# The first mixture of a two-layer float32 kernel: one gather for two experts' first 64 rows, layer two in four column quarters on partition strips, and the spread by strips

## The chip, the cores and the metric

The kernel runs on one core of a Trainium2 chip. The metric is the time of one execution on the device, in microseconds; lower is better. Four engines matter here: TensorE (PE in the profile) multiplies matrices, VectorE (DVE) and ScalarE (ACT) work element by element, SyncE (SP) issues the loads of the weights. Matrices are float32 all through.

## What is computed

Two transformer-like blocks in a row on 256 tokens of width 1024. The first ends with a mixture of 32 experts, and this mixture is all that the change touches:

```python
def moe_ffn(h, w_router, b_router, w1, b1, w2, b2):      # T = 256 tokens, D = 1024
    top_v, top_e = lax.top_k(logits, TOP_K)              # 4 of 32 experts a token
    weights = jax.nn.softmax(top_v, axis=-1)
    ...
    def expert_block(args):                              # the rows of one expert
        tok, e = args
        hcat = x_pad[tok] @ w1[e] + b1[e]                # 1024 -> 2048, "layer one"
        x_glu = jnp.minimum(hcat[:, ::2], SWIGLU_LIMIT)
        x_lin = jnp.clip(hcat[:, 1::2], -SWIGLU_LIMIT, SWIGLU_LIMIT)
        act = x_glu * jax.nn.sigmoid(SWIGLU_ALPHA * x_glu) * (x_lin + 1.0)
        return act @ w2[e] + b2[e]                       # 1024 -> 1024, "layer two"
    ...
    out = jnp.sum(y[dest].reshape(T, TOP_K, D) * weights[..., None], axis=1)
```

How many of the 256 tokens an expert gets is known only from the data; with the inputs here no expert gets more than 96.

## The kernel before, in words

`tensor_moe1` is the TensorE part of the first mixture. It loops over the experts u = 0 to 31, written out one after another in the program. An expert's rows are taken in passes of 32 rows. The code of four passes (128 rows) is in the program for every expert; passes two, three and four stand in `If(count > 32)`, `If(count > 64)`, `If(count > 96)`, where `count` is loaded into a register of TensorE (L914). Where an `If` is not taken, TensorE branches over the code of the further passes. `either` (L746) adds an `Else` that raises the semaphore, `only` (L736) has none.

For one expert TensorE does, in this order:

- **Layer one, half 0**: bias through a 32x32 matmul (L874, four), then 16 matmuls (L881) of 32 rows by 512 columns, four strips of 32 PSUM partitions wide; they use chunks 0 and 1 of w1. The further passes' code follows in an `If`. **Half 1** is the same with chunks 2 and 3, without bias.
- **The spread of expert u - 1** (`spread1`, `spread`, L481): four matmuls of 128 x 512 add the expert's rows back to the tokens, each row times its weight; four more (L843) in an `If(count > 64)` for rows 64 to 127. VectorE adds the eight PSUM tiles into `YV` (`vector_spread`, L1748).
- **at**: two transpositions (L906) of the activation that VectorE has made out of layer one (L1825 to L1835, with the sigmoid of ScalarE, L2389).
- **The gather of expert u + 1** (`gather`): four transpositions of the weighted selection (L800, tile `swt`) and 16 matmuls of 128 x 128 (L481, tile `hg`) that pick the expert's rows, up to 128, out of the normalised tokens. ScalarE copies the results to SBUF (L2351, L2368).
- **Layer two**: 16 matmuls (L893) of 32 rows by 512 columns for pass 0, the further passes in `If`s (L962 and below). ScalarE copies each pass's result to SBUF in two pieces of 64 x 512 (L2400, `evict`, all four passes always).

SyncE loads six chunks of 2 MB an expert (four of w1, two of w2) into a ring of eight slots, in program order. A slot is loaded anew when TensorE has freed its last chunk (semaphores `s_pe`, `s_px`, `s_py`).

In both programs TensorE's instructions stand in memory in the order of the code, with all bodies of `If`s between them.

## Time and profile before

| | before |
|---|---|
| time of three executions, us | 2183.54, 2178.27, 2179.35 (median 2179.35) |
| span of the profiled execution, first to last instruction, us | 2180.7 |
| TensorE busy, share of the span | 83% |
| mean granted TensorE clock | 0.927 |
| first mixture's experts, us from the span's start | about 392 to 1397 |
| weights loaded for them | 192 loads of 2048 KB |

The profile gives no time of the profiled execution beside its span; the span lies 1.35 us above the median of the three executions, so that a sum made in the span's microseconds can be taken over to the median with that shift. A timeline row reads: start, duration, engine, line, operation, tiles, shapes, number of records, and in brackets how long the engine had stood idle ahead of it and what it waited for.

### The profile page before, as it was taken

The page shows a single profiled execution, that of the slowest core. Times are in us where ns is not written, and L with a number is a line of the kernel's source. Part 1 is how long each engine was busy: PE and PEld are TensorE (multiplying, and loading weights), DVE is VectorE, ACT ScalarE, POOL GpSimd, SP SyncE. Part 2 cuts the span into 40 slices and gives each one's busy share as a digit, 9 for nine tenths or more (in the row PEclk, how much of TensorE's full clock was granted, in tenths as well). Part 3 has the DMA queues.
Part 4 walks back from the last instruction along what each step waited for, and adds up shares of the span by engine and source line. Part 5 has one row for each costly group of instructions (what it writes and reads, how often), then busy time and mean ns, then how long its engine had stood idle before and what let it go on. Part 6 is the DMA issues. An engine that isn't in the chain of part 4 may idle for free. (4 is left out here: it accounts for less than half of the span.)

```text
span 2180.7 us, 28331 instructions
## 1 busy us (share of the span) xinstructions
PE 1818.2 (83%) x11496; PEld 831.2 (38%) x11496; DVE 806.8 (37%) x1613; ACT 506.2 (23%) x1028; POOL 77.0 (4%) x96
## 2 busy tenths in 40 slices
PE   7899999999999988989977898599989855565556
PEld 3654445433333433434333243255534522222221
DVE  2215533333342434534444344488882200000001
ACT  2022311232331233332333333222410200000000
POOL 0000000000000000000000000085000000000000
PEclk9999999999999999999999999799999878877888
DMA  7835349789897799999999999534228299999997
GB/s 268 301 133 195 136 173 376 316 367 409 342 420 311 309 425 423 422 423 402 425 422 423 423 424 423 189 121 142 91 102 345 96 429 428 427 428 428 428 427 320
DMA packets 114821, 713.56 MB, mean 327 GB/s; under 512 B 16799, under 2 KB 21102, under 8 KB 69006
## 3 DMA queue, kind: packets, MB, share of 16 engines
q1 hardware_dynamic: 106208, 704.98, 79.3%
q10 hardware_dynamic: 8398, 5.47, 0.9%
q8 instruction: 165, 2.70, 0.5%
q14 instruction: 50, 0.41, 0.1%
HBM read 709.35 MB, written 1.07 MB: 326 GB/s over the span
## 5 line engine op out<-in xcount | busy, mean ns | idle before, releaser
L881 PE MATMUL ps<-ring,ar 128*32 128x512 f32 x3072 | 368.3, 620 | 41.7 <-DMA ring<-in_w 18.4
L481 PE MATMUL ps<-ar 128*128 128x128 f32 (+5 forms) x1742 | 351.2, 359 | 41.0 <-PEq L755 20.5
L488 PE MATMUL ps<-ring,ar 128*32 128x512 f32 x1184 | 196.0, 691 | 138.0 <-DMA ring<-in_w_gate 45.3
L481 PEld LDWEIGHTS ps<-ar 128*128 128x128 f32 (+2 forms) x1742 | 234.1, 200 | 160.5 <-issue 121.8
L481 PE MATMUL ps<-ring,ar 128*128 128x512 f32 (+2 forms) x592 | 248.8, 580 | 3.8 <-DVE ar L1423 1.7
L881 PEld LDWEIGHTS ps<-ring,ar 128*32 128x32 f32 x3072 | 99.3, 113 | 307.5 <-issue 279.9
L1825 DVE TENSOR_SCALAR ar<-ps 128x256 f32<-128x256 f32 x128 | 54.4, 425 | 403.8 <-PE ps L881 395.0
L893 PE MATMUL ps<-ring,ar 128*32 128x512 f32 x1536 | 175.0, 602 | 0.0
L596 PE MATMUL ps<-ring,ar 128*128 128x512 f32 x384 | 170.2, 594 | 0.0
L481 PEld LDWEIGHTS ps<-ring,ar 128*128 128x128 f32 x592 | 113.2, 193 | 132.8 <-issue 127.0
L2400 ACT ACTIVATE ar<-ps 64x512 f32<-64x512 f32 x256 | 151.3, 591 | 46.6 <-PE ps L893 33.4
L1748 DVE TENSOR_TENSOR ar<-ps,ar 128x512 f32<-128x512 f32 x176 | 121.7, 692 | 101.6 <-PE ps L481 91.2
L488 PEld LDWEIGHTS ps<-ring,ar 128*32 128x32 f32 x1184 | 55.7, 125 | 246.2 <-issue 245.3
L488 PE MATMUL ps<-ar 128*32 128x512 f32 x288 | 112.2, 703 | 37.6 <-DMA ring<-in_w_up 21.8
L2389 ACT ACTIVATE ar<-ar 128x256 f32<-128x256 f32 x128 | 53.3, 416 | 315.8 <-DVE ar L1825 309.8
L1835 DVE TENSOR_TENSOR ar<-ar 128x256 f32<-128x256 f32 x128 | 79.5, 621 | 97.5 <-ACT ar L2389 90.7
L2437 ACT ACTIVATE ar<-ps 128x256 f32<-128x256 f32 x128 | 49.0, 383 | 256.9 <-PE ps L906 208.0
L2124 DVE TENSOR_TENSOR ar<-ps,ar 128x512 f32<-128x512 f32 x8 | 5.5, 692 | 262.0 <-ACT ar L2576 262.0
L596 PEld LDWEIGHTS ps<-ring,ar 128*128 128x128 f32 x384 | 71.2, 191 | 79.8 <-issue 79.4
L893 PEld LDWEIGHTS ps<-ring,ar 128*32 128x32 f32 x1536 | 46.5, 111 | 101.3 <-issue 101.3
L2368 ACT ACTIVATE ar<-ps 128x512 f32<-128x512 f32 x80 | 47.8, 597 | 94.9 <-PE ps L481 94.9
L874 PE MATMUL ps<-ar 32*32 32x512 f32 x384 | 53.8, 617 | 15.2 <-PEq L973 10.5
(403 smaller groups left out, 1385.8 us busy)
## 6 DMA issues: line engine op xcount, KB each, us to landing
ring<-in_w SPq DMA_DIRECT2D x192, 2048.0 KB, 20.0
ring<-in_w_gate SPq DMA_DIRECT2D x25, 2048.0 KB, 29.4
ring<-in_w_up SPq DMA_DIRECT2D x25, 2048.0 KB, 31.4
ring<-in_w_down SPq DMA_DIRECT2D x24, 2048.0 KB, 30.1
ring<-in_w_in SPq DMA_DIRECT2D x21, 2048.0 KB, 8.7
ring<-in_w_ada SPq DMA_DIRECT2D x12, 2048.0 KB, 8.5
ar<-in_w_up SPq DMA_DIRECT2D x7, 2048.0 KB, 29.2
ar<-in_w_gate SPq DMA_DIRECT2D x7, 2048.0 KB, 29.6
```

The lines of the kernel that those rows point to most:

```text
L481: ins = self.t.e.matmul(o, l, r, start=(i == 0), stop=(i == len(pairs) - 1))
L488: ins = self.t.e.matmul(b[32 * i:32 * i + 32, :], l, r, start=(k == 0), stop=(k == len(steps) - 1))
L596: ins = t.e.matmul(b[:, :], HV[:, k, TB(tb)], W[:, k, :], start=(k == 0), stop=(k == 7))
L874: e.matmul(b[32 * s:32 * s + 32, :], pick, B1R[:, HALF(s)], start=True, stop=False)
L881: ins = e.matmul(b[32 * s:32 * s + 32, :], HG[:, 2 * c + r, 32 * n:32 * n + 32], W[:, r, HALF(s)], start=False, stop=(c == 3 and r == 1))
L893: ins = e.matmul(b[64 * h + 32 * r:64 * h + 32 * r + 32, :], AT_[:, 2 * s + r, 32 * n:32 * n + 32], W[:, s % 2, r, HALF(h)], start=(s == 0 ...
L1748: k = v(v.own.tensor_tensor(o, b, o, ALU.add))
L1825: dve["glu", u, n] = v(v.own.tensor_scalar(glu, b[:, 0:512:2], 7.0, None, ALU.min))
L1835: dve["ac", u, n] = v(v.own.tensor_tensor(o, lin.rearrange("p (q r) -> p q r", r=2), sg.rearrange("p (q r) -> p q r", r=2), ALU.mult))
L2389: act["sg", u, n] = s(s.own.activation(M[:, 512:768], M[:, 0:256], ACT.Sigmoid, scale=1.702))
L2400: k = s(s.own.activation(YG_[n // 2][64 * (n % 2):64 * (n % 2) + 64, HALF(h)], ps("l2", u, n)[64 * h:64 * h + 64, :], ACT.Copy))
L2437: m = s(s.own.activation(o, ps("at", u, k)[:, 256 * i:256 * i + 256].rearrange("p (r s n) -> p r s n", r=2, s=4), ACT.Copy))
```

## The change

Layer two of a pass writes four column quarters of 256 onto the four strips of 32 partitions of one PSUM bank (32 matmuls of 256 columns in place of 16 of 512), so ScalarE evicts a pass with one copy of 128 x 256. The spread multiplies strip by strip: for every pass eight matmuls of 32 rows deep by 256 columns wide, passes two to four in `If`s, and it stands between the two halves of layer one in place of behind them. For the weights, a selection is turned by matmuls of 32 x 128 that write each pass onto all four strips (`turned_picks`). The gather is made once for two experts, for 64 rows of each (`gather_pair`, in odd experts only); rows 64 to 127 are gathered in an `If(count > 64)` inside the expert itself (`rest`). VectorE picks two experts ahead, and adds the spread at the start of an expert, ahead of its four activation steps; ScalarE copies what `rest` made for every expert, taken or not. The activation has one buffer (`ATB`) in place of two.

```diff
-    ATB = [A(2048 + 1024 * i, 8, 128) for i in range(2)]
-    ACB, YG_ = A(4096, 4, 256), [A(5120 + 1024 * i, 1024) for i in range(2)]
-    SB = [A(7168 + 256 * i, 2, 128) for i in range(2)]
-    SWB = A(7680, 2, 2, 128)
-    SWT = [A(8192 + 512 * i, 2, 256) for i in range(2)]
-    TM = [A(9216 + 768 * i, 768) for i in range(2)]
+    ATB = A(2048, 8, 128)
+    ACB, YG_ = A(3072, 4, 256), A(4096, 4, 256)
+    SB = [A(5120 + 512 * i, 2, 2, 128) for i in range(2)]
+    SWB = [A(6144 + 256 * i, 2, 128) for i in range(2)]
+    SWT = [A(6656 + 1024 * i, 4, 256) for i in range(2)]
+    TM = [A(8704 + 768 * i, 768) for i in range(2)]
+    HGR = A(10240, 8, 64)
...
-    TL1X = (7, 0)
+    QUART = (4, 5, 6, 7)
...
-    def gather_weights(t, w, m, u, lane):
-        b = w.claim("swt", m, u, lane=lane)
-        t.wait_ge(s_dve, dve["sel", m, u])
-        for i in range(2 if m == 1 else 1):
+    def turned_picks(t, b, u, passes):
+        for i, n in enumerate(passes):
             for tb in range(2):
-                ins = t.e.transpose(b[:, TB(2 * i + tb)], (SWB, SWB2)[m - 1][:, i, tb, :], ident)
-        pe["swt", m, u] = t(ins)
-    def gather_rows(t, w, m, u, lane):
-        t.wait_ge(s_dve, dve["pick", m, u])
-        t.wait_ge(s_act, act["rows", m])
+                for q in range(4):
+                    ins = t.e.matmul(b[32 * q:32 * q + 32, TB(2 * i + tb)], SWB[u % 2][:, tb, 32 * n:32 * n + 32],
+                                     ident, start=True, stop=True)
+        return ins
+    def gather_pair(t, w, p, h, lane):
+        t.wait_ge(s_dve, dve["pick", 1, 2 * p + 1])
+        t.wait_ge(s_act, act["rows", 1])
+        b = w.claim("hg", 1, p, h, lane=lane)
+        for k in range(4):
+            n = w.sums(b[:, TB(k)], [(XNV[:, tb, TB(4 * h + k)], SB[p % 2][:, :, tb, 0:64]) for tb in range(2)])
+        pe["hg", 1, p, h] = n
+    def gather_turned(t, w, u, lane):
+        b = w.claim("swt", 1, u, lane=lane)
+        t.wait_ge(s_dve, dve["sel", 1, u])
+        pe["swt", 1, u] = t(turned_picks(t, b, u, (0, 1)))
...
     def tensor_moe1(t, w):
         e = t.e
         tensor_route(t, w, 1, WR1, 32, 128)
-        gather_rows(t, w, 1, 0, TL1)
-        gather_weights(t, w, 1, 0, TL1)
+        for h in range(2):
+            gather_pair(t, w, 0, h, (TL1[h],))
+        gather_turned(t, w, 0, (6,))
...
         def spread1(u, count):
-            spread(t, w, 1, u, TL1)
-            def second_half():
-                t.wait_ge(s_act, act["yg", 1, u, 1])
+            banks4 = [w.claim("sp", 1, u, q, lane=(QUART[q],)) for q in range(4)]
+            def rows(n):
+                t.wait_ge(s_act, act["yg", 1, u, n])
                 for tb in range(2):
-                    for h in range(2):
-                        b = w.claim("sp", 1, u, 1, tb, h, lane=TL1X)
-                        psp[u, tb, h] = z(e.matmul(b[:, :], SWT[u % 2][:, 1, TB(tb)], YG_[1][:, HALF(h)], start=True,
-                                                   stop=True))
-            either(t, z, count, 64, second_half)
-            psp["all", u] = z.n
+                    for q in range(4):
+                        g = slice(32 * q, 32 * q + 32)
+                        ins = e.matmul(banks4[q][:, 256 * tb:256 * tb + 256], SWT[u % 2][g, n, TB(tb)], YG_[g, n, :],
+                                       start=(n == 0 and tb == 0), stop=True, skip_group_check=True)
+                return ins
+            def third():
+                only(t, count, 96, lambda: rows(3))
+                rows(2)
+            def second():
+                only(t, count, 64, third)
+                z(rows(1))
+            pe["sp", 1, u] = t(rows(0))
+            either(t, (z,), count, 32, second)
+            psp[u] = z.n
...
+            def rows_of(k, n):
+                if n < 2:
+                    c0 = 64 * (u % 2) + 32 * n
+                    return HGB[u // 2 % 2][:, k, c0:c0 + 32]
+                return HGR[:, k, 32 * n - 64:32 * n - 32]
...
+            def layer2(b, n, halves, arrive, first):
 
                 for s in range(4):
+                    if s // 2 not in halves:
+                        continue
                     if arrive and s % 2 == 0:
                         w.weights("w2", u, s // 2)
                     W = RG_(slot["w2", u, s // 2], 0, 2, 2, 1024)
-                    for h in range(2):
-                        for r in range(2):
-                            ins = e.matmul(b[64 * h + 32 * r:64 * h + 32 * r + 32, :],
-                                           AT_[:, 2 * s + r, 32 * n:32 * n + 32], W[:, s % 2, r, HALF(h)],
-                                           start=(s == 0), stop=(s == 3))
+                    for r_ in range(2):
+                        for q in range(4):
+                            ins = e.matmul(b[32 * q:32 * q + 32, 0:256], ATB[:, 2 * s + r_, 32 * n:32 * n + 32],
+                                           W[:, s % 2, r_, 256 * q:256 * q + 256], start=(s == 0 and r_ == 0),
+                                           stop=(s == 3 and r_ == 1))
...
+                def rest():
+                    b = w.claim("hr", u, lane=(3,))
+                    for k in range(8):
+                        for tb in range(2):
+                            e.matmul(b[:, 64 * k:64 * k + 64], XNV[:, tb, TB(k)], SB[u // 2 % 2][:, u % 2, tb, 64:128],
+                                     start=(tb == 0), stop=(tb == 1))
+                    b = w.claim("sr", u, lane=(2,))
+                    r(turned_picks(t, b, u, (2, 3)))
 
                 def further(n):
                     if half == 0:
                         w.claim("l1", u, n, lane=(n,))
-                    return layer1(ps("l1", u, n), n, half, False)
+                    return layer1(ps("l1", u, n), n, chunks, False)
 
                 def third():
+                    t.wait_ge(s_act, act["rest", u])
                     only(t, count, 96, lambda: further(3))
                     further(2)
 
                 def second():
+                    if half == 0:
+                        either(t, (r,), count, 64, rest)
+                        w.claim("l1", u, 1, lane=(1,))
+                    b1 = ps("l1", u, 1)
+                    layer1(b1, 1, chunks[0:1], False)
                     only(t, count, 64, third)
-                    x(further(1))
-                either(t, x, count, 32, second)
-                for c in (2 * half, 2 * half + 1):
+                    x(layer1(b1, 1, chunks[1:2], False))
+                either(t, (x, r), count, 32, second)
+                if half == 0:
+                    pr["rest", u] = r.n
+                for c in chunks:
                     w.free("w1", u, c)
                     px["free", "w1", u, c], py["free", "w1", u, c] = x.n, 0
+                if half == 0 and u > 0:
...
+                    spread1(u - 1, counts[u - 1])
             px["l1", u] = x.n
-            if u > 0:
-                spread1(u - 1, counts[u - 1])
             if u == LATE_BIAS:
                 biases()
-            pe["at", u, 0] = t(turn_act(0, (0,)))
+            further_pair = u % 2 == 1 and u + 1 < NE
             if u + 1 < NE:
-                gather(t, w, 1, u + 1, TL1)
-            turn_act(1, (1,))
+                gather_turned(t, w, u + 1, (5,))
+            if further_pair:
+                gather_pair(t, w, u // 2 + 1, 0, (6,))
+            pe["at", u, 0] = t(turn_act(0, (0,), 4))
+            if further_pair:
+                gather_pair(t, w, u // 2 + 1, 1, (4,))
             t.wait_ge(s_act, act["at", u, 0])
 
             def first_second(ins):
@@ -947,30 +1013,26 @@
             def first_third(ins):
                 px["at", u, 2] = x(ins)
 
-            pe["l2", u, 0] = t(layer2(w.claim("l2", u, 0, lane=(7,)), 0, True, first_second))
+            b = w.claim("l2", u, 0, lane=(7,))
+            layer2(b, 0, (0,), True, None)
+            turn_act(1, (1,), 5)
...
+            pe["l2", u, 0] = t(layer2(b, 0, (1,), True, first_second))
...
+    def vector_quarters(v, u):
+        v.wait_ge(s_pe, pe["sp", 1, u])
+        v.wait_ge(s_ps, psp[u])
+        for q in range(4):
+            o = YV[:, :, 256 * q:256 * q + 256]
+            b = ps("sp", 1, u, q).rearrange("p (b n) -> p b n", b=2)
+            if u == 0:
+                v(v.own.tensor_copy(o, b))
+            else:
+                v(v.own.tensor_tensor(o, b, o, ALU.add))
+            read["sp", 1, u, q] = v.mark()
...
         for u in range(NE):
             if u + 1 < NE:
-                vector_pick(v, 1, u + 1)
                 vector_select(v, 1, u + 1)
+            if u + 2 < NE:
+                vector_pick(v, 1, u + 2)
+            if u > 0:
+                vector_quarters(v, u - 1)
...
-                if n == 0 and u > 0:
-                    vector_spread(v, 1, u - 1)
-                    if u == LATE_BIAS:
-                        biases()
-        vector_spread(v, 1, NE - 1)
+                if n == 0 and u == LATE_BIAS:
+                    biases()
+        vector_quarters(v, NE - 1)
...
+    def scalar_rest(s, u):
+        s.wait_ge(s_pr, pr["rest", u])
+        if u > 0:
+            s.wait_ge(s_px, px["l1", u - 1])
+        if u > 1:
+            s.wait_ge(s_pe, pe["sp", 1, u - 2])
+            s.wait_ge(s_ps, psp[u - 2])
+        s(s.own.activation(HGR, ps("hr", u).rearrange("p (k s) -> p k s", k=8), ACT.Copy))
+        read["hr", u] = s.mark()
+        act["rest", u] = s(s.own.activation(SWT[u % 2][:, 2:4, :], ps("sr", u).rearrange("p (n q) -> p n q", n=2),
+                                            ACT.Copy))
+        read["sr", u] = s.mark()
...
-            for h in range(2):
-                k = s(s.own.activation(YG_[n // 2][64 * (n % 2):64 * (n % 2) + 64, HALF(h)],
-                                       ps("l2", u, n)[64 * h:64 * h + 64, :], ACT.Copy))
+            act["yg", 1, u, n] = s(s.own.activation(YG_[:, n, :], ps("l2", u, n)[:, 0:256], ACT.Copy))
...
         for u in range(NE):
+            scalar_rest(s, u)
             sigmoid(u, 0)
+            if u + 1 < NE:
+                scalar_gather_turned(s, u + 1)
+            if u % 2 == 1 and u + 1 < NE:
+                scalar_gather_pair(s, u // 2 + 1, 0)
             turned_act(s, u, 0, (0,))
-            if u + 1 < NE:
-                scalar_gather(s, 1, u + 1, l1, lambda: sigmoid(u, 1))
-            else:
-                sigmoid(u, 1)
+            sigmoid(u, 1)
+            if u % 2 == 1 and u + 1 < NE:
+                scalar_gather_pair(s, u // 2 + 1, 1)
             turned_act(s, u, 1, (1,))
             for n in (2, 3):```

TensorE in expert 1 before, from the end of layer one's half 1 to the first pass of layer two (L752 the Else of layer one, L481 of 128x512 the spread, L843 its second half, L906 the turned activation, L800 `swt`, L481 of 128x128 the gather `hg`, L893 layer two):

```order
L752 UNCONDITIONAL_BRANCH
L481 MATMUL ps<-ar 128x512 x4
L748 COMPARE_AND_BRANCH
L843 MATMUL ps<-ar 128x512 x4
L748 UNCONDITIONAL_BRANCH
L752 UNCONDITIONAL_BRANCH
L906 MATMUL ps<-ar 128x128 x2
L800 MATMUL ps<-ar 128x128 x4
L481 MATMUL ps<-ar 128x128 x16
L906 MATMUL ps<-ar 128x128 x2
L893 MATMUL ps<-ring,ar 32x512 x16
```

TensorE in expert 1 after, between layer one's half 0 (ends with the two branches of L749 and L753) and half 1 (L922), where L869 is the spread:

```order
L753 UNCONDITIONAL_BRANCH
L869 MATMUL ps<-ar 128x256 x8
L749 COMPARE_AND_BRANCH
L741 COMPARE_AND_BRANCH x2
L869 MATMUL ps<-ar 128x256 x8
L741 UNCONDITIONAL_BRANCH
L869 MATMUL ps<-ar 128x256 x8
L741 UNCONDITIONAL_BRANCH
L869 MATMUL ps<-ar 128x256 x8
L749 UNCONDITIONAL_BRANCH
L753 UNCONDITIONAL_BRANCH
L922 MATMUL ps<-ring,ar 32x512 x16
```

The spread has moved up from behind half 1 to between the halves, and is one group of eight and three more in nested `If`s where it was four and four. TensorE in expert 1 after, from layer one's end to layer two (L803 the turned selection, L482 the gather for two experts, L949 the turned activation, L936 layer two):

```order
L753 UNCONDITIONAL_BRANCH
L803 MATMUL ps<-ar 32x128 x16
L482 MATMUL ps<-ar 128x128 x8
L949 MATMUL ps<-ar 128x128 x2
L482 MATMUL ps<-ar 128x128 x8
L936 MATMUL ps<-ring,ar 32x256 x16
L949 MATMUL ps<-ar 128x128 x2
L936 MATMUL ps<-ring,ar 32x256 x16
L749 COMPARE_AND_BRANCH
```

Between layer one and the turned activation there stands the gather's first part, and the second turned activation has moved into the middle of layer two, whose matmuls are 32 in place of 16. TensorE in expert 1 after, from the start of layer one's half 0 to the end of its `If`s' first part (L915 bias, L965 and L803 of `rest`):

```order
L915 MATMUL ps<-ar 32x512 x4
L922 MATMUL ps<-ring,ar 32x512 x16
L749 COMPARE_AND_BRANCH x2
L965 MATMUL ps<-ar 128x64 x16
L803 MATMUL ps<-ar 32x128 x16
L749 UNCONDITIONAL_BRANCH
L753 UNCONDITIONAL_BRANCH
L915 MATMUL ps<-ar 32x512 x4
L922 MATMUL ps<-ring,ar 32x512 x8
```

Where before the further passes followed at once, the body of `rest` now stands ahead of them; the four further groups of layer two, counted like this through one expert, make 368 matmuls in the program on average (360 in even, 376 in odd experts), where the expert had 244.

## Rows read from the trace of the kernel before

**Rows 1.** The page: queue with instructions (packets, MB, share); loads (KB each, us to landing)

```profile
q8 instruction: 165, 2.70, 0.5%
...
ring<-in_w SPq DMA_DIRECT2D x192, 2048.0 KB, 20.0
```

**Rows 2.** Windows: busy us and (records) of each engine, PEclk, DMA share, GB/s

```profile
390.00:740.00 350.00, 331.36 (x2669) 129.16 (x2667) 126.67 (x264) 97.66 (x190) 0.00 (x0) 1.00 0.86 356
740.00:1372.00 632.00, 552.29 (x3934) 226.32 (x3926) 258.83 (x535) 206.05 (x403) 0.00 (x0) 0.95 1.00 419
```

**Rows 3.** Instruction groups, 385 to 1400 us: busy us, mean ns, idle before

```profile
L881 PE MATMUL ps<-ring,ar 128*32 128x512 f32 x3072 | 368.3, 620 | 41.7 <-DMA ring<-in_w 18.4 <-issue 12.3 <-PEq L755 10.7
...
L481 PE MATMUL ps<-ar 128*128 128x512 f32 x256 | 130.4, 653 | 27.7 <-PEq L755 20.5 <-ACT ar L2400 3.6 <-ACT ar L2389 2.7
...
L881 PEld LDWEIGHTS ps<-ring,ar 128*32 128x32 f32 x3072 | 99.3, 113 | 307.5 <-issue 279.9 <-DMA ring<-in_w 27.3
```

**Rows 4.** TensorE's waits, 385 to 1400 us: total, times, longest

```profile
PE ps L874 <- PEq L973: 10.5, 4, 2.9
```

**Rows 5.** TensorE timeline of expert 23 (its start to that of expert 24)

```profile
1120.51 1.06 PE L874 MATMUL ps<-ar 32*32 32x512 f32 x8 [2.85 <-PEq L973]
...
1126.21 3.64 PE L881 MATMUL ps<-ring,ar 128*32 128x512 f32 x32 [1.07 <-PEq L755]
1131.87 5.37 PE L481 MATMUL ps<-ar 128*128 128x512 f32 x8 [2.03 <-PEq L755]
...
1138.03 3.84 PE L481 MATMUL ps<-ar 128*128 128x128 f32 x32
...
1142.35 3.64 PE L893 MATMUL ps<-ring,ar 128*32 128x512 f32 x32
1145.92 1.06 PE L874 MATMUL ps<-ar 32*32 32x512 f32 x8
```

**Rows 6.** TensorE timeline in expert 24 and at its end

```profile
1149.40 3.62 PE L881 MATMUL ps<-ring,ar 128*32 128x512 f32 x26 [1.43 <-issue]
1156.06 5.34 PE L881 MATMUL ps<-ring,ar 128*32 128x512 f32 x32 [3.04 <-PEq L755]
1161.98 1.09 PE L481 MATMUL ps<-ar 128*128 128x512 f32 x2 [0.58 <-PEq L755]
```

**Rows 7.** TensorE timeline: first and last of twelve pairs of stalls

```profile
425.49 3.64 PE L881 MATMUL ps<-ring,ar 128*32 128x512 f32 x32 [0.57 <-PEq L755]
431.40 1.10 PE L481 MATMUL ps<-ar 128*128 128x512 f32 x2 [2.27 <-PEq L755]
...
1336.73 5.34 PE L881 MATMUL ps<-ring,ar 128*32 128x512 f32 x32 [4.26 <-PEq L755]
1342.61 0.67 PE L481 MATMUL ps<-ar 128*128 128x512 f32 x1 [0.54 <-PEq L755]
```

**Rows 8.** TensorE timeline: starts of experts 1, 2, 10, 11 and 31

```profile
420.29 1.06 PE L874 MATMUL ps<-ar 32*32 32x512 f32 x8
...
443.75 1.06 PE L874 MATMUL ps<-ar 32*32 32x512 f32 x8
...
739.49 1.06 PE L874 MATMUL ps<-ar 32*32 32x512 f32 x8
...
766.21 1.06 PE L874 MATMUL ps<-ar 32*32 32x512 f32 x8 [2.15 <-PEq L973]
...
1355.58 1.06 PE L874 MATMUL ps<-ar 32*32 32x512 f32 x8
```

**Rows 9.** TensorE timeline: matmuls 32 rows deep, and of 256 columns

```profile
1508.52 1.17 PE L481 MATMUL ps<-ring 32*128 32x256 f32 x16
...
1609.07 1.93 PE L488 MATMUL ps<-ring 128*32 128x256 f32 x32
```

**Rows 10.** TensorE timeline, the last spread of the first mixture

```profile
1390.27 6.48 PE L481 MATMUL ps<-ar 128*128 128x512 f32 x8 [3.59 <-ACT ar L2400]
```

**Rows 11.** The chain that ended last, VectorE behind expert 31's sums

```profile
1398.02 2.96 issue
```

More of the change, by code:

```diff
@@ L1132, in tensor_moe2 @@
         tensor_route(t, w, 2, W36, 36, 32)
-        gather(t, w, 2, 0, TL2)
+        gather(t, w, 0, TL2)
         for u in range(NE // 4):
@@ L2373, in scalar_moe1 @@
+            read["hg", 2, u, h] = s.mark()
+        act["hg", 2, u] = n
     def scalar_moe1(s):
```

238 lines of the change are left out of this document (113 added, 125 removed).

## The prediction

> **What bounds the kernel now.** The change touches the first mixture alone, so I read its stretch, 385 to 1400 us, by windows, by groups, by waits, and then expert by expert on TensorE. The windows show two parts [rows 2]. From 390 to 740 us the DMA share is 0.86 and TensorE is busy for 331 of 350 us. From 740 to 1372 us the DMA share is 1.00 at 419 GB/s, and TensorE is busy for 552 of 632. There the loads set the pace: six of 2048 KB [rows 1] at 419 GB/s are 30.0 us an expert, and experts 11 to 31 start 589.4 us apart over 20 experts, 29.5 each [rows 8]. TensorE has some 80 us to spare in this part.
>
> The groups and the waits ask for a second look. Little of TensorE's idle time is for data (18.4 us for weights); 20.5, 10.7 and 10.5 us are its sequencer behind the `Else`s of L755 and L973, and 12.3 us are "issue" in the middle of layer one [rows 3, 4]. A branch does not explain the latter: no branch stands there. What does is where they stand. Layer one's 48 passes of 32 matmuls left 3072 MATMUL and 3072 LDWEIGHTS records [rows 3], so a matmul is four queue entries and a transposition two; an expert before is 244 matmuls (12 of them transpositions) and some 20 branches, 977 entries. Counted in these entries along the program, all eight gaps inside layer one (the one at 1149.40 is one) [rows 6] lie at the same place modulo 256. The page has a queue that moved 165 packets of instructions, 2.70 MB [rows 1], 16.4 KB each, 64 bytes times 256. And walking TensorE's program with the branches that this data takes touches 165 blocks of 256 entries. So TensorE's program comes in blocks of 256 entries, and an engine that enters a block early waits for it.
>
> How long a block takes is seen where two stalls follow each other over one block boundary: from one resumption to the next there is one block. Expert 23 resumes at 1120.51, 1126.21 and 1131.87: 5.70 and 5.66 us; expert 24 at 1149.40, 1156.06 and 1161.98: 6.66 and 5.92 [rows 5, 6]. Over twelve such pairs in the stretch, of which the first and the last stand in [rows 7] with 5.91 and 5.88, the mean is 6.1. The packets share the DMA engines with the loads; VectorE's jump at the end of the stretch, with few loads under way, shows 2.96 us [rows 11], which I take for the low end.
>
> **The change part by part, as work.** The spread before costs 130.4 us for 32 experts, 4.1 each [rows 3]. Sixteen records 32 rows deep and 256 columns wide took 1.17 us [rows 9], so after it is 1.2 a pass, 1.8 an expert: -2.3. The gather was 3.84 an expert [rows 5], after it is half as often: -1.9. Layer two takes 3.64 a pass [rows 5]; 64 records of 256 columns are twice 1.93 [rows 9]: +0.2. `rest` adds a gather of 3.8 for three-pass experts alone (5), and ahead of their third pass a wait for two ScalarE copies. Net TensorE work falls by 3 to 4 us in a one-pass expert, and rises by 1 in a three-pass one. In the part from 740 on the loads hide that saving. Before 740 the DMA engines stand still for 0.14 of 350 us [rows 2], 49 us, mostly beside the experts of three passes, whose work does not fall: I count -4. Behind expert 31 the spread falls from 6.48 [rows 10] to 1.2 us, and its copies and sums shorten with it: -9. VectorE's and ScalarE's edits (picks two ahead, sums first, one copy a pass, the two copies of `rest` always) lie beside TensorE; if that cover were gone they would cost the sums' 2.8 us at the start of an expert. Work alone gives 2181 - 4 - 9 + 1 = 2169.
>
> **The change as program.** Per expert the code grows from 244 to 368 matmuls, 977 to 1486 entries, 3.8 to 5.8 blocks: +64 blocks in 32 experts. Not taken bodies are skipped. Before, no jump was over 245 entries, less than a block, so nothing was ever passed by. After, a one-pass expert jumps over 92 matmuls (376 entries) in half 0 and over 100 (400) behind layer two. Such a jump passes a whole block in (376-255)/256 and (400-255)/256 of cases, together 1.0 an expert, for 21 one-pass experts 21 blocks. So 165 + 64 - 21 = 208 blocks.
>
> A one-pass expert thus walks 4.8 blocks in place of 3.8. At 6.1 us that is 23.2 us before; the five in the first part took 23.5 to 26.7, mean 25.1 (the first and the last of them in [rows 8]), so the surplus over the fetch is 1.9. After, 4.8 x 6.1 = 29.3, and with 1.7 of surplus 31.0. That is over the 29.5 of the loads: from there on the instructions, not the weights, set the pace. Two-pass experts enter the `If`s and jump shorter, 5.7 blocks, 35 us; three-pass ones walk 5.6, 34 us, hidden under some 48 us of work.
>
> The Trainium skill, page "Runtime: NRT & Kernel Launch", section "Instruction fetch mechanics", gives blocks of 256 instructions, purely sequential prefetch, and a stall where a taken branch leaves the two blocks at hand. The trace agrees with the 256 [rows 1]; no jump before is long enough to show the stall. By its rule of the jump the sum would be the one below. The same section calls the crossing of a block mostly hidden, by which it would be that of rival 1; the resumptions in [rows 5, 6] say otherwise.
>
> The sum, by parts:
> - Experts 0 to 10: five of one pass, 31.0 in place of 25.1, +29; four of three passes +2 each (1 of work, 1 of the wait for `rest`), +8; the two of two passes 0.
> - Experts 11 to 30: 15 x 31.0 + 4 x 35 + 48.5 = 653 in place of 589: +64.
> - The end: -9 of work, +4 for one more block: -5.
> Together +96 on a span of 2180.7, which is 1.35 above the median: 2275.
>
> Bounds. With 5.7 us a block, the short end of the pairs, a one-pass expert takes 29.1: the parts are +20 + 8 + 36 - 6 (two-pass experts at 35 still) and the time 2237; with no surplus 27.4, the loads' 29.5 bind again, and the parts are +12 + 8 + 17 - 6 (two- and three-pass experts alone are longer) and the time 2210. If the block that is jumped over has been asked for already and must land first, up to 5.8 blocks count; in half the cases that is +3 us in 21 experts, less what overlaps, +50: 2325. I take 6.1, the mean of the pairs, since the loads after are as dense as before.
>
> **The rivals.**
> 1. Faster, by the work. Block arrival is hidden, or a jump is served as quickly as a fall-through. For it: TensorE stood idle only some 55 us for its sequencer over the whole stretch [rows 3, 4]. Against: three resumptions 5.7 us apart in one expert [rows 5]. It gives 2169, 0.5% faster. It decides if a block takes under 3 us, as in [rows 11]. Chance 0.08.
> 2. No change. A block takes 3 to 4.5 us; a one-pass expert then stays under the loads' 29.5, the work's -12 is eaten by the stalls after far jumps (21 x 0.5 to 1 us). 2180, within 6. For it: the loads bound 632 us of the stretch. Chance 0.07.
> 3. Slower, but less: 5 to 5.7 us a block, because TensorE's longer waits leave the loads gaps in which blocks come sooner. 2215 to 2245. Chance 0.25.
> 4. My forecast, 2245 to 2310. Chance 0.45.
> 5. Slower still: the far jump waits for the block in flight and then for its own. 2310 to 2350. Chance 0.15.
>
> **How the numbers follow.** The likeliest is 2275. The range 2215 to 2335 leaves out rivals 1 and 2 (0.15) and the outer part of 5 (0.05), 2 in 10. A difference under 0.3% cannot be told from none here. Faster 0.08, same 0.07, slower 0.85.
>
> **What would show it.** The instruction queue: 165 packets become about 208 (up to 229 if passed blocks are fetched too), 2.70 MB becomes 3.4. One-pass experts start 29 to 33 us apart, before 740 and behind. TensorE's busy share from 740 on falls below 0.8, the DMA share below 1.00, and the idle time in front of the spread, of half 1 and of the next expert's bias is put down to the sequencer or to "issue", some 3 times as much as before. The last spread takes under 2 us. If the packets rise and the spacing does not, the 6.1 us is not what an early engine waits for, and the prediction falls; if the packets stay at 165, the count of blocks does.

## The result, and the profile after

| | before | after |
|---|---|---|
| median (lowest to highest), us | 2179.28 (2178.27 to 2183.54) | 2322.29 (2313.18 to 2327.66) |
| ratio after to before, 95% interval | | 1.0641 (1.0615 to 1.0668) |
| span of the profiled execution, us | 2180.7 | 2319.3 |
| first TensorE work behind the mixture, us | 1408.45 | 1547.89 |

The changed kernel is 6.4% slower by the ratio, and the medians lie 143 us apart (6.6%, inside the interval). The whole loss lies in the first mixture: the next stage's first work on TensorE comes 139.4 us later, of 138.6 us of span.

The page after: TensorE's busy time, the granted clock in 40 slices, and the queue that brings instructions (packets, MB, share).

```profile
PE 1794.5 (77%) x14208; PEld 862.2 (37%) x14208; DVE 772.2 (33%) x1529; ACT 423.6 (18%) x932; POOL 77.4 (3%) x96
...
PEclk9999998899989989879987789879999987787787
...
q8 instruction: 228, 3.74, 0.6%
```

Where [rows 1] had 165 packets there are 228, one under the upper figure of the prediction (229) and 20 above its likeliest (208), and TensorE's share has fallen from 83% to 77% though it executes more. The windows after (columns as in [rows 2]):

```profile
390.00:740.00 350.00, 289.37 (x3284) 135.84 (x3287) 100.59 (x207) 65.28 (x144) 0.00 (x0) 0.92 0.80 320
740.00:1360.00 620.00, 465.19 (x4766) 204.96 (x4758) 204.47 (x413) 125.56 (x281) 0.00 (x0) 0.87 0.89 361
```

From 740 us on TensorE's share is 0.75 and the DMA share 0.89, where [rows 2] had 0.87 and 1.00: the loads no longer set the pace, and no wait of TensorE for a load is left in the stage. The groups and then the waits of the stage (us in total, times, longest) say what does:

```profile
L922 PE MATMUL ps<-ring,ar 128*32 128x512 f32 x3072 | 409.8, 675 | 27.1 <-issue 14.3 <-PEq L758 12.8
...
L915 PE MATMUL ps<-ar 32*32 32x512 f32 x384 | 66.5, 749 | 102.4 <-PEq L758 96.7 <-issue 5.7
...
L869 PE MATMUL ps<-ar 32*128 32x256 f32 x768 | 67.4, 481 | 58.8 <-PEq L758 37.4 <-issue 15.7 <-ACT ar L2514 5.7
```

```profile
PE ps L915 <- PEq L758: 96.7, 24, 6.0
PE ps L869 <- PEq L758: 37.4, 13, 4.7
...
PE ps L869 <- issue: 15.7, 6, 3.5
PE ps L803 <- issue: 15.6, 5, 4.0
PE ps L922 <- issue: 14.3, 10, 2.8
```

All waits of TensorE for its sequencer and "issue" in the stage add up to 208 us (10 rows, of which these are the largest) against 59 before (7 rows, [rows 3, 4] have the largest). They stand in front of the next expert's bias (L915, behind the skip of layer two's further passes), of the spread (L869, behind the skip in half 0), and, as "issue", in the middle of straight code. The end of expert 16 and the whole of expert 17 on TensorE's timeline, both of one pass:

```profile
1010.75 2.21 PE L936 MATMUL ps<-ring,ar 128*32 128x256 f32 x32
1018.44 1.93 PE L915 MATMUL ps<-ar 32*32 32x512 f32 x8 [5.49 <-PEq L758]
1020.30 4.90 PE L922 MATMUL ps<-ring,ar 128*32 128x512 f32 x32
1028.75 1.19 PE L869 MATMUL ps<-ar 32*128 32x256 f32 x16 [3.54 <-PEq L758]
1029.87 1.06 PE L922 MATMUL ps<-ring,ar 128*32 128x512 f32 x1
1032.99 5.38 PE L922 MATMUL ps<-ring,ar 128*32 128x512 f32 x31 [2.06 <-issue]
1040.86 1.08 PE L803 MATMUL ps<-ar 128*32 128x128 f32 x32 [2.49 <-PEq L758]
...
1049.30 1.93 PE L936 MATMUL ps<-ring,ar 128*32 128x256 f32 x32
1055.62 1.93 PE L915 MATMUL ps<-ar 32*32 32x512 f32 x8 [4.39 <-PEq L758]
```

Read it as in [rows 5]. Expert 17 resumes at 1018.44, then at 1028.75 behind the long skip of half 0, 10.3 us later, where a pair before took 6.1; then at 1032.99 in straight code and at 1040.86 behind half 1's skip. It takes 37.2 us, of which the engine works about 24. The row of 1018.44 shows a second thing: eight records that take 1.06 us [rows 5] took 1.93 behind a wait of 5.49. The stretch's granted clock is 0.92 and 0.87 (PEclk in the windows) where it was 1.00 and 0.95 [rows 2], and layer one's 3072 records rose from a mean of 620 ns [rows 3] to 675. What the engine did ahead of this slow row is wait; the clock is examined below.

The end of the stage:

```profile
1532.15 2.09 PE L869 MATMUL ps<-ar 32*128 32x256 f32 x16 [5.75 <-ACT ar L2514]
1547.89 3.67 PE L571 MATMUL ps<-ar 128*128 128x128 f32 x16 [13.65 <-DVE ar L1461]
```

The last spread took 2.09 us where [rows 10] had 6.48, and from the start of expert 31 to the next stage's first work it is 47.6 us where it was 52.9.

### The profile page after: what moved, and what is told of

Read it like the earlier page. It is cut to its first block and busy times, and to the rows that moved or that the text cites. A ratio compares the mean times of both kernels' runs of the same rounds, so it can differ in the third digit from the quotient of the medians.

```text
span 2319.3 us, 33403 instructions
## 1 busy us (share of the span) xinstructions
PE 1794.5 (77%) x14208; PEld 862.2 (37%) x14208; DVE 772.2 (33%) x1529; ACT 423.6 (18%) x932; POOL 77.4 (3%) x96
## 3 DMA queue, kind: packets, MB, share of 16 engines
q8 instruction: 228, 3.74, 0.6%
HBM read 709.35 MB, written 1.07 MB: 306 GB/s over the span
## 5 line engine op out<-in xcount | busy, mean ns | idle before, releaser
L922 PE MATMUL ps<-ring,ar 128*32 128x512 f32 x3072 | 409.8, 675 | 27.1 <-issue 14.3
L489 PE MATMUL ps<-ring,ar 128*32 128x512 f32 x1184 | 193.9, 685 | 142.0 <-DMA ring<-in_w_gate 46.4
L1829 DVE TENSOR_TENSOR ar<-ps,ar 128x512 f32<-128x512 f32 x124 | 85.7, 691 | 498.2 <-PE ps L869 416.4
L482 PE MATMUL ps<-ring,ar 128*128 128x512 f32 (+2 forms) x592 | 246.7, 576 | 3.5 <-DVE ar L1485 1.7
L922 PEld LDWEIGHTS ps<-ring,ar 128*32 128x32 f32 x3072 | 103.5, 122 | 327.4 <-issue 327.2
L936 PE MATMUL ps<-ring,ar 128*32 128x256 f32 x3072 | 188.8, 394 | 11.7 <-ACT ar L2514 11.7
L482 PE MATMUL ps<-ar 128*128 128x128 f32 (+6 forms) x974 | 172.6, 338 | 26.3 <-ACT ar L2514 13.7
L482 PEld LDWEIGHTS ps<-ring,ar 128*128 128x128 f32 x592 | 112.3, 191 | 131.3 <-issue 125.7
L482 PEld LDWEIGHTS ps<-ar 128*128 128x128 f32 (+3 forms) x974 | 135.5, 214 | 64.0 <-issue 36.6
L489 PEld LDWEIGHTS ps<-ring,ar 128*32 128x32 f32 x1184 | 54.2, 124 | 250.2 <-issue 249.3
L915 PE MATMUL ps<-ar 32*32 32x512 f32 x384 | 66.5, 749 | 102.4 <-PEq L758 96.7
L936 PEld LDWEIGHTS ps<-ring,ar 128*32 128x32 f32 x3072 | 95.8, 113 | 83.0 <-ACT ar L2514 16.0
L869 PE MATMUL ps<-ar 32*128 32x256 f32 x768 | 67.4, 481 | 58.8 <-PEq L758 37.4
L2182 DVE TENSOR_TENSOR ar<-ps,ar 128x512 f32<-128x512 f32 x8 | 5.5, 692 | 263.0 <-ACT ar L2653 263.0
L869 PEld LDWEIGHTS ps<-ar 32*128 32x128 f32 x768 | 48.3, 228 | 90.1 <-issue 79.6
L2514 ACT ACTIVATE ar<-ps 128x256 f32<-128x256 f32 x128 | 49.2, 384 | 150.4 <-PE ps L936 90.0
## 6 DMA issues: line engine op xcount, KB each, us to landing
ring<-in_w SPq DMA_DIRECT2D x192, 2048.0 KB, 13.0
ring<-in_w_gate SPq DMA_DIRECT2D x25, 2048.0 KB, 29.4
ring<-in_w_up SPq DMA_DIRECT2D x25, 2048.0 KB, 31.4
ring<-in_w_down SPq DMA_DIRECT2D x24, 2048.0 KB, 30.1
ring<-in_w_in SPq DMA_DIRECT2D x21, 2048.0 KB, 8.1
ring<-in_w_ada SPq DMA_DIRECT2D x12, 2048.0 KB, 8.6
ar<-in_w_up SPq DMA_DIRECT2D x7, 2048.0 KB, 30.4
ar<-in_w_gate SPq DMA_DIRECT2D x7, 2048.0 KB, 29.4
```

Source lines behind the costliest of these rows:

```text
L482: ins = self.t.e.matmul(o, l, r, start=(i == 0), stop=(i == len(pairs) - 1))
L489: ins = self.t.e.matmul(b[32 * i:32 * i + 32, :], l, r, start=(k == 0), stop=(k == len(steps) - 1))
L869: ins = e.matmul(banks4[q][:, 256 * tb:256 * tb + 256], SWT[u % 2][g, n, TB(tb)], YG_[g, n, :], start=(n == 0 and tb == 0), stop=True, ski ...
L915: e.matmul(b[32 * s:32 * s + 32, :], pick, B1R[:, HALF(s)], start=True, stop=False)
L922: ins = e.matmul(b[32 * s:32 * s + 32, :], rows_of(2 * c + r_, n), W[:, r_, HALF(s)], start=False, stop=(c == 3 and r_ == 1))
L936: ins = e.matmul(b[32 * q:32 * q + 32, 0:256], ATB[:, 2 * s + r_, 32 * n:32 * n + 32], W[:, s % 2, r_, 256 * q:256 * q + 256], start=(s == ...
```

## The experiments

The first four were run side by side (median of the kernel before 2179.47 us), the others in two later groups (2181.66 and 2181.60). `only(t, count, 96, ...)` is a body that no expert here executes. The first three pad the kernel before with matmuls in such bodies.

**pad_near: 64 matmuls an expert that are never executed, no skip longer than a block**

```diff
+                def padding():
+                    for _ in range(55):
+                        e.matmul(ps("sp", 1, u, 1, 0, 0)[:, :], SWT[u % 2][:, 1, TB(0)], YG_[1][:, HALF(0)], start=True,
+                                 stop=True)
                 for tb in range(2):
                     for h in range(2):
                         b = w.claim("sp", 1, u, 1, tb, h, lane=TL1X)
+                        if tb == 0 and h == 0:
+                            only(t, count, 96, padding)
...
             def fourth():
+                b3 = w.claim("l2", u, 3, lane=(3,))
+                for _ in range(9):
+                    e.matmul(b3[0:32, :], AT_[:, 0, 96:128], RG_(slot["w2", u, 0], 0, 2, 2, 1024)[:, 0, 0, HALF(0)],
+                             start=True, stop=True)
...
```

> The kernel before with 64 more matmuls an expert in the program that are never executed (they stand under a condition of over 96 rows), placed so that no branch skips more than 245 entries: one block of 256 entries more an expert, no work more. Theory one (TensorE's instructions come in blocks of 256 entries, one after the other, some 5 to 6 us each): instruction packets 165 + 32 = 197, a one-pass expert walks 4.8 blocks, some 30 us, the time is 50 to 100 us above before. Rival (the changed kernel is slower by its work, its waits or the narrower matmuls, and the length of the program costs nothing): no change, 2179 within 6.

Measured: 2240.86 us against 2179.47, ratio 1.0296 (1.0272 to 1.0320), so +61 us.

```profile
q8 instruction: 197, 3.23, 0.6%
```

197 packets, as worked out. Instructions that are never executed cost 61 us; the rival falls. The bias rows of the timeline give each expert's start: the 20 one-pass experts from 1 to 30 are now 29.4 us apart on average, where they were 26.3.

**pad_far: the same 64, all in half 0's body of pass four**

```diff
                     if half == 0:
                         w.claim("l1", u, n, lane=(n,))
+                        for _ in range(64 if n == 3 else 0):
+                            e.matmul(ps("l1", u, n)[0:32, :], pick, B1R[:, HALF(0)], start=True, stop=False)
```

> The same 64 matmuls an expert, but all in one body that is always skipped, so that one branch an expert skips 501 entries and nearly always passes a whole block. Theory one with passed blocks fetched all the same: 197 packets, and as slow as the other placing or slower (60 to 120 us above before), since the jump waits for the block under way and then for its own. Theory one without such a fetch: 166 packets, and only the exposed time behind the jump, 20 to 60 us above before. Rival: no change.

Measured: 2305.36 us, ratio 1.0589 (1.0567 to 1.0611), +126 us, just above the 60 to 120 that I gave.

```profile
q8 instruction: 194, 3.18, 0.6%
```

The same number of packets within three, and twice the price: the block that is passed is fetched all the same, and it is not the number of blocks alone that counts but where they lie. The starts of the experts show where the second half of the price arises. One-pass experts, which skip the padding with everything else, are 29.8 us apart, hardly more than with the near placing (29.4). Two-pass experts (without expert 0) take 39.9 us in place of 33.7 and three-pass experts 52.0 in place of 47.0: they stop in front of a further pass of half 0, where the skip of the padding lands (14 waits of L874 put down to "issue", 40.1 us in all, 3.9 before). The eleven experts of two and three passes hold 61 of the 70 us by which the two placings differ between the starts of experts 0 and 31.

**pad_full: 124 matmuls an expert, skips as long as after's.** The same three places with 32 (half 0), 44 (spread) and 48 (layer two).

> The kernel before with 124 never executed matmuls an expert, as many as the change adds, and with skips of about the same lengths (377, 195, 200 and 405 entries): the work of before in a program as long as after. Theory one: 229 packets as after has 228, and 120 to 170 us above before, that is within 30 of after. Rival: no change, 2179 within 6.

Measured: 2327.37 us, ratio 1.0698 (1.0668 to 1.0729), +148 us; the changed kernel is at +143. Its queue and layer one's group:

```profile
q8 instruction: 227, 3.72, 0.6%
```

```profile
L889 PE MATMUL ps<-ring,ar 128*32 128x512 f32 x3072 | 405.9, 676 | 43.8 <-PEq L755 37.6 <-issue 6.2
```

This is the central run. It does the work of before, with the tiles, copies and waits of before, in a program as long as after's, and has after's time within 5 us and its packets (227). Layer one's records also have after's mean (676 ns, after 675). Its granted clock fell too, but less than after's: 0.95 and 0.92 in the two windows, where before had 1.00 and 0.95 and after has 0.92 and 0.87.

```profile
390.00:740.00 350.00, 302.95 (x2310) 114.00 (x2304) 111.90 (x235) 89.16 (x173) 0.00 (x0) 0.95 0.81 322
740.00:1360.00 620.00, 500.98 (x3390) 200.41 (x3382) 227.25 (x469) 170.62 (x335) 0.00 (x0) 0.92 0.90 366
```

So waits for instructions alone lowered the clock here, by 0.05 and 0.03 where the changed kernel lost 0.08 in both windows. That the rest of the fall is no cause of its own is not shown; before_no34 and after_no34 below come back to it.

**after_no4: the changed kernel without pass four's matmuls**

```diff
-                only(t, count, 96, lambda: rows(3))
                 rows(2)
...
-                    return layer1(ps("l1", u, n), n, chunks, False)
+                    return layer1(ps("l1", u, n), n, chunks, False) if n < 3 else None
...
-                layer2(w.claim("l2", u, 3, lane=(3,)), 3, (0, 1), False, None)
+                w.claim("l2", u, 3, lane=(3,))
```

> The changed kernel without the matmuls of pass four (rows 96 to 127, which no expert has with these inputs, so nothing that is executed is left out): 292 matmuls an expert in place of 368, 4.6 blocks in place of 5.8, and skips of 296 and 272 entries in place of 376 and 400. Theory one: packets 228 - 38 = 190, one-pass experts 28 to 30 us apart, the time 2180 to 2225. Rival (work, waits or narrow matmuls): nothing changes, 2322 within 8.

Measured: 2202.33 us, ratio 1.0110 (1.0093 to 1.0127).

```profile
q8 instruction: 190, 3.11, 0.6%
```

120 us of the 143 are gone with code that no expert executes; 190 packets, as worked out. One-pass experts are 27.4 us apart (28 to 30 expected). Three-pass experts still take 50.4 us, where before has 47.3: the shorter program does not take these 3 us each, 16 in all, back. `rest` alone is 4.9 us of work in each of them (L965 and L803, at 547.12 us in the changed kernel's expert 4).

**after_split: the long skips cut in two**

```diff
-                    if half == 0:
-                        either(t, (r,), count, 64, rest)
-                        w.claim("l1", u, 1, lane=(1,))
...
+                if half == 0:
+                    either(t, (r,), count, 64, rest)
-                either(t, (x, r), count, 32, second)
+                either(t, (x,), count, 32, second)
...
-                either(t, (y,), count, 64, third)
-            either(t, (x, y), count, 32, second)
+            either(t, (x,), count, 32, second)
+            either(t, (y,), count, 64, third)
```

> The changed kernel with the same matmuls in the same order, but its two long skips cut in two: the gather of rows 64 to 127 and the rest of half 0's further passes stand under two conditions one after the other (128 and 245 entries), and so do pass two and passes three and four of layer two (about 140 and 261). Same work, same length of program, some branches more. Theory one (blocks of 256 entries; passing a block costs its fetch and then the fetch of the next one): 228 packets as before the cut, and the time falls by 40 to 80 us, to about 2260, since the two paddings differed by 65 us for that reason alone. Rival (only the number of blocks fetched counts): 2322 within 10. Rival (work and waits): 2322, or a little above for the branches.

Measured: 2331.60 us, ratio 1.0686 (1.0658 to 1.0714): 9 us above the changed kernel, which was measured in another group; the intervals of the two ratios overlap at their edges, so that a loss is not certain. The 40 to 80 less that I had expected are ruled out. In this kernel the length of a skip as such has no price that cutting it takes away. **after_no4_split** is the same cut in the kernel without pass four:

> The changed kernel without pass four's matmuls and with its long skips cut in two as well: 4.6 blocks an expert, no skip over 255 entries. Theory one: 190 packets, one-pass experts at 27 to 29 us, so that the loads set the pace from 740 us on again: 2165 to 2185, against 2202 with the long skips. Rival (only the number of blocks counts): 2202 within 6.

Measured: 2212.13 us, ratio 1.0141 (1.0118 to 1.0165), 10 us above after_no4, with intervals that overlap, and outside both the 2165 to 2185 and the rival's 2202 within 6: the same miss. **pad_far_split** puts the padding of pad_far behind half 0 under a condition of its own:

```diff
                 either(t, x, count, 32, second)
...
+                if half == 0:
+                    only(t, count, 96, padding)
```

> The padding of 64 never executed matmuls an expert behind half 0, under a condition of its own, so that the one skip of 501 entries becomes two, of 245 and 258, that follow each other at once. If a long skip has a price of its own (the rule that a branch beyond the two blocks at hand must ask anew): about 2240, as the near placing. If what counts is that two blocks in a row hold no work, so that the time of the second block is not covered by anything (the theory left after the changed kernel did not gain by the same cut): 2305 within 12, as the far placing, with 194 to 197 packets.

Measured: 2290.57 us, ratio 1.0500 (1.0467 to 1.0534), 15 us below pad_far and 50 above pad_near. Just outside the 12 us that I gave, and far from 2240. Its largest wait on TensorE (us in total, times, longest):

```profile
PE ps L881 <- issue: 136.4, 37, 9.9
```

Single waits reach 9.9 us, more than any block took before. That fits two blocks in a row with no work between them, the second of which is asked for when the engine lands in the first. But the cut also moved the padding behind the further passes of half 0, and the starts of the experts show both effects: three-pass experts fall from 52.0 to 46.8 us and two-pass ones from 39.9 to 36.7, while one-pass experts rise from 29.8 to 31.4. So the 15 us gained are those of a better place, and do not speak for shorter skips.

**pad_jump: one skip over eight blocks among loads, one behind them**

```diff
                 t.wait_ge(s_act, act["yg", 1, u, 1])
+                for _ in range(512 if u in (15, NE - 1) else 0):
+                    e.matmul(ps("sp", 1, u, 0, 0, 0)[:, :], SWT[u % 2][:, 1, TB(0)], YG_[1][:, HALF(0)], start=True,
+                             stop=True)
```

> The kernel before with 512 never executed matmuls (2048 entries, eight blocks) in the skipped body of one spread among dense loads (that of expert 15's rows) and 512 in the last one, where few loads run. It reads off the price of one block directly. If every passed block is fetched in turn: 165 + 16 = 181 packets, some 8 x 5.5 = 44 us of stall in expert 16 and 8 x 3 = 24 us behind the last spread. If only the next block is fetched ahead and the engine then goes to the target: 165 to 167 packets and stalls of at most 12 and 6 us.

Measured: 2188.57 us, ratio 1.0032 (1.0014 to 1.0049). The queue, and TensorE at the skip, which stands between the spread (L481) and the turned activation (L909) of expert 16:

```profile
q8 instruction: 169, 2.77, 0.5%
```

```profile
916.98 7.07 PE L884 MATMUL ps<-ring,ar 128*32 128x512 f32 x64
926.41 5.37 PE L481 MATMUL ps<-ar 128*128 128x512 f32 x8 [2.35 <-PEq L755]
935.62 0.41 PE L909 MATMUL ps<-ar 128*128 128x128 f32 x2 [3.84 <-PEq L755]
```

Four packets more: that is two above what I gave for fetching one block ahead, and far from 16. Eight blocks are not fetched one after the other. The engine resumes at 926.41 and, behind the skip, at 935.62: 9.2 us, in place of the 5.7 to 6.7 of [rows 5, 6]. The whole of expert 16 took 31.9 us where it took 24.9 before, so the 3 us more at the skip are not all that this expert lost. Behind the last spread no stall showed: the next work on TensorE, which waits 11.5 us for VectorE there anyway, was not held up. The reading that fits, from this one skip, is that a long skip costs the rest of the block under way and then the target's.

**after_spread_late: the spread behind half 1 again.** `spread1` is called behind the loop over the halves, and `vector_quarters(v, u - 1)` behind the first activation step.

> The changed kernel with the spread behind half 1 of layer one again and VectorE's sums behind the first activation step, as before the change; everything else as changed. Theory one: the same blocks and skips in another place, so 228 packets and 2322 within 15. Rival (the spread between the halves holds up layer one, or the sums ahead of the activation do): 10 to 40 us faster than the changed kernel.

Measured: 2365.17 us, ratio 1.0858 (1.0828 to 1.0888), 43 us slower than the changed kernel, outside both expectations. The packets stay at 228; what is new stands in the waits:

```profile
PE ps L915 <- PEq L758: 67.0, 23, 5.7
PE ps L803 <- DVE ar L1829: 58.4, 27, 5.9
```

The turned selection (L803) writes bank 5, which the spread has just filled, and waits 27 times for VectorE's sums (L1829). Between the halves that wait is covered. So the move does not undo one part; it adds a wait, and with four banks for the spread the new place is the better one.

**before_no4: the kernel before without pass four's matmuls** (the same edit as in after_no4, in `further` and `fourth`)

> The kernel before without the matmuls of pass four, which these inputs never execute: 192 matmuls an expert in place of 244, 3.0 blocks in place of 3.8. Theory one: 165 - 26 = 139 packets, TensorE's sequencer and issue waits fall from some 50 us to under 15; but from 740 us on the loads set the pace, so only the first part and the end gain: 2165 to 2177. Rival (the fetch costs the kernel before nothing): 2179 within 4.

Measured: 2165.92 us, ratio 0.9934 (0.9915 to 0.9952), faster than both kernels. Its queue, and two of TensorE's waits in the stage:

```profile
q8 instruction: 138, 2.26, 0.4%
```

```profile
PE ps L881 <- DMA ring<-in_w: 66.4, 30, 4.5
...
PE ps L481 <- PEq L755: 1.4, 2, 1.2
```

The waits for the sequencer are gone (20.5 us in front of L481 in [rows 3], 1.4 now), and TensorE waits 66.4 us for loads where it waited 18.4. The kernel before lost some 14 us (0.66% of 2180) to instructions too.

**before_no34 and after_no34: both kernels without TensorE's matmuls of passes three and four.** Rows 64 to 127 are left out, so that five experts have less work. Both leave out the same passes, but the kernel before still gathers 128 rows an expert, while in the changed one `rest` is empty: its cost in three-pass experts is not in this comparison.

```diff
-                    return layer1(ps("l1", u, n), n, half, False)
+                    return layer1(ps("l1", u, n), n, half, False) if n < 2 else None
...
-                y(layer2(w.claim("l2", u, 2, lane=(2,)), 2, False, None))
+                w.claim("l2", u, 2, lane=(2,))
+                y(e.nop())
```

> The kernel before without TensorE's matmuls of passes three and four (rows 64 to 127, of which five experts have some: this part of the computation is left out): 132 matmuls an expert, 2.1 blocks. Theory one: no sequencer waits, some 107 packets, the loads set the pace all through: 2130 to 2155.

> The changed kernel without the same matmuls of passes three and four: 180 matmuls an expert, 2.9 blocks, some 132 packets. With both kernels free of the instruction supply, the difference to the kernel before cut in the same way is the price of the change's work and waits alone. Theory one: 3 to 14 us faster than that kernel, by the shorter end of the stage (the first rival of the prediction, without the length of the program). Rival (the change's work, waits or narrow matmuls are part of why it is slower): slower than that kernel.

Measured: 2124.78 us (ratio 0.9743, 0.9721 to 0.9765) and 2130.06 us (0.9760, 0.9737 to 0.9783): the intervals overlap. The first lies below the 2130 to 2155 that I gave, the second is not the 3 to 14 us faster; the packets are 111 and 136, where I had 107 and 132. TensorE's waits in the stage, before_no34 first, then after_no34:

```profile
PE ps L880 <- DMA ring<-in_w: 78.1, 37, 4.3
```

```profile
PE ps L921 <- DMA ring<-in_w: 131.7, 67, 4.4
...
PE ps L914 <- PEq L758: 2.8, 4, 1.3
```

With both free of the instruction supply (2.8 us of sequencer waits are left in the second), the change gives TensorE 54 us more to wait for loads, and no time. The next stage starts at 1350.89 against 1354.43, 3.5 us earlier, which the medians do not show. For experts of one and two passes this is what the change does without its length: nothing that can be measured here.

The clock differs all the same. The windows from 740 to 1340 us, before_no34 first:

```profile
740.00:1340.00 600.00, 497.92 (x3503) 198.26 (x3496) 243.44 (x503) 192.82 (x377) 0.00 (x0) 0.94 1.00 418
```

```profile
740.00:1340.00 600.00, 452.20 (x4790) 187.61 (x4782) 231.71 (x464) 139.77 (x316) 0.00 (x0) 0.90 1.00 418
```

With next to no waits for instructions the change lowers the granted clock from 0.94 to 0.90, and layer one's records rise from a mean of 622 ns to 670. So part of the changed kernel's lower clock comes from the change and not from the length of its program. Here it costs no time, as the loads set the pace (DMA share 1.00 in both). Whether TensorE's longer waits or its narrower matmuls bring it about was not tested, nor what it costs where instructions set the pace; pad_full, 5 us above the changed kernel without it, leaves little room for it.

## Why the prediction was right, and where it was off

The time lay inside the range (2215 to 2335), the sign and the cause were as forecast; the likeliest figure, 2275, was 47 us short, and the case that came true is the fifth (2310 to 2350), the far jump that waits for the block in flight, to which I gave 0.15. My own case, passed blocks that are never fetched, did not come true.

- **The count of blocks** held only with the passed blocks in it: 228 packets, where the sum went by 208 and the bound had 229. The step "165 + 64 - 21" took 21 blocks off for being jumped over, and they were fetched. Counted with them, 197, 194, 227, 190 and 138 packets in the padded and shortened kernels stand against 197, 197, 229, 190 and 139 worked out.
- **The price of a block**, 6.1 us between resumptions, held as an order of size: 5.8 blocks in 32.8 us are 5.7 each. It cannot be simply multiplied: 32 blocks with work between them cost 61 us (pad_near), as many in one place 126 (pad_far).
- **The failed term** is the one-pass expert, "4.8 x 6.1 = 29.3, and with 1.7 of surplus 31.0". The 20 one-pass experts from 1 to 30 start 32.8 us apart (27.3 to 37.5), where they were 26.3 apart; the missing 1.8 us each are 36 of the 47 us. I left the passed block out of the count except in the bounds. What it costs is seen against pad_near, whose one-pass experts walk the same 4.8 blocks and pass none: they take 29.4 us and not 31.0. So the term was 1.6 us too dear for the blocks that it counted, and the passed block, put at nothing, cost 3.4 us; the two errors partly cancelled, and that the figure came within 47 us is in part luck. pad_jump's single skip agrees in size (9.2 us between resumptions in place of about 6), as does the 3 us of my upper bound.
- **Three-pass experts** take 50.5 us (mean of five, 47.3 before), where I had 48.3 for four and 48.5 for one: 11 us in all; after_no4 has 50.4 too, which points to the change's own work and waits, that I had put at 2 us, and not to the length of the program. Two-pass experts did not rise (33.4 to 32.9, expert 0 included), where I had 35 for four of them and no change for expert 6: 7 us the other way. Expert 1 begins 3.5 us later, which I had not in the sum. In the span the miss is 42.6 us (2319.3 against 2180.7 + 96), and 36 + 11 - 7 + 3.5 makes 43.5; the rest of the 47 is that the span now lies 3.0 us under the median and before 1.4 above it.
- **The end** came as worked out: -5.3 against -5, though the last spread took 2.09 us and not 1.2, and so not under 2.
- **The bound at 2210** does not come out of its parts: 15 x 29.5 + 4 x 35 + 48.5 is 631, 42 over 589 and not 17. The 29.5 is the mean of all experts there, while the one-pass ones were 26.7 apart. The range did not rest on it.
- **Rival one**, the work alone at 2169, is what before_no34 and after_no34 test: the saving is there on TensorE, and not in the time, since the loads bind. The two kernels show 3.5 us at the stage's end where that rival had 12 (13 off and 1 on), with three-pass rows left out of both.
- **Rival two** (3 to 4.5 us a block) fell with pad_near, and rival three with the result; the upper end of rival three's price, 5.7 us a block, is what came, but for 5.8 blocks an expert and not 4.8.

What stays open: that the next block is asked for when the engine enters the one before it fits the pairs and the waits of up to 9.9 us in pad_far_split, but was inferred from resumptions; no record shows a request. Nor is it settled if the cut costs the changed kernel anything, and why one-pass experts with the same 4.8 blocks take 29.4, 29.8 and 31.4 us in pad_near, pad_far and pad_far_split. And what a block takes with no loads beside it was not measured: the skip behind the last spread was hidden.

Of the Trainium skill's page "Runtime: NRT & Kernel Launch", section "Instruction fetch mechanics": its rule that a taken branch beyond the two blocks at hand forces a fetch of the target agrees with pad_jump (9.2 us), and its word that crossing a block is mostly hidden does not hold where a block is gone through in less than the 6.1 us that the next one takes.

## What to carry to other kernels

In a fully written-out program with conditions, count instructions as well as work: divide the program's entries by 256, take the blocks that each unit of work walks or skips (a single skipped block was fetched too), and compare them times the time between resumptions (6 us here) with the unit's own time. The queue of instruction packets on the page and a column of idle time "issue" in straight code are the signs. Bodies that are nearly never executed are paid for on every pass by them, and twice as dearly in pad_far, where they stood in one place ahead of code that was still to run; taking out pass four, which these inputs never reach, gained 0.7% in the kernel before and 5% in the changed one, while the change's own saving of TensorE work was worth nothing measurable under loads that already set the pace.

## What the hardware did that I had not expected

- Cutting a skip of over a block into two skips within a block does not help (2331.60 against 2322.29 us).
- A skip over eight blocks costs no more than one over a single block: 9.2 us between resumptions in pad_jump, 10.3 in expert 17 of the changed kernel.
- Waiting for instructions also lowered the granted clock: from 740 us on it was 0.92 in pad_full in place of 0.95, and layer one's records took 676 ns in place of 620, with no change of the matmuls. The change lowers it as well without such waits (0.94 to 0.90 between before_no34 and after_no34).
